# State-space half of an output projection beside an attention: 512 columns of one token tile in eight half pieces, where it was 256 columns of both tiles

## Chip, cores and metric

One core of one Trainium2 chip. The metric is the device time of one launch in microseconds (us), the median of several runs. Engines: TensorE (PE in the profile, its weight loads apart as PEld), VectorE (DVE), ScalarE (ACT), GpSimd (POOL) and SyncE (SP), which issues the weight loads from HBM.

## What is computed

Two transformer blocks on 256 tokens of width 1024. The second block's mixer is the one that matters here:

```python
u = h @ w_in[l]
y_ssd = ssd_mixer(u_ssd, ...)            # 256 x 1024, state-space half
y_mla = mla_mixer(u_mla, positions, ...) # 256 x 1024, 16-head latent attention
x = x + jnp.concatenate([y_ssd, y_mla], axis=-1) @ w_out[l]   # w_out: 2048 x 1024
x = x + memory_attention(rmsnorm(x, ...), rmsnorm(mem, ...), ...)
```

The product with `w_out` is split by rows. Rows 0 to 1023 meet `y_ssd` (layer `out_ssd` of the kernel), rows 1024 to 2047 meet `y_mla` (layer `out_mla`). `y_ssd` is ready before the attention runs, so `out_ssd` can be computed between the steps of the attention.

## The kernel before

**Numbers.** A float32 product is made of three reduced-precision products: `product` (L2253) issues hi x hi (L2256), hi x lo (L2257) and lo x hi (L2258). The stationary operand (128 x 128) is a k tile of the tokens of one token tile, the moving operand is a stretch of a weight row tile. The 256 tokens are two tiles t of 128; the 1024 rows are eight k tiles r.

**Weights** come in units of 2048 elements per partition, in one global order (`LAYERS`), through a ring of three raw buffers. For each unit k SyncE issues two loads, ScalarE rounds it to `w_hi` (`split`, the instruction at L687, semaphore `rounded`) and VectorE forms `w_lo = raw - w_hi` (L1494, semaphore `resid`). TensorE waits for `resid >= k + 1` before it uses unit k, and signals `unit_used` with the last matmul on it. The rounded copies too live in three buffers: the four units of `out_ssd`, 96 to 99, lie in buffers 0, 1, 2, 0 and the first two of `out_mla` in 1, 2. ScalarE must see a buffer's last unit used before it rounds the next one into it. Below, unit 0 to 3 means the four of `out_ssd`.

**Order.** Each engine's order is written out by hand. TensorE, around the change (L3005 to L3018):

```python
scores(0)
out_ssd(0, 0)
out_ssd(0, 1)
for gi in range(3):
    scores(gi + 1)
    turn_probs(gi)
    out_ssd(gi + 1, 0)
    weighted(gi)
    out_ssd(gi + 1, 1, (lambda: turn_probs(3)) if gi == 2 else None)
weighted(3)
```

Four groups gi of four heads: `scores` (L2636, 16 records), the softmax on ScalarE (`exps`, L953) and VectorE (`row_max` L1769 and L1771, `attn_factors` L1793 and L1798), `turn_probs` (transposes, L2649, 12 records), a copy from PSUM (`prob_T_out`, L1787), `weighted` (L2666, 16 records), a copy (`attn_out`, L1805). `scores(gi)` waits for the exponentials of gi - 1, `turn_probs(gi)` for `rec_ready` of `attn_factors(gi)`, `weighted(gi)` for `prob_T_out(gi)`.

`out_ssd(i, t)` (L2671) computes 256 columns of token tile t over all eight k tiles with unit i alone: 24 matmuls of 256 columns into one half of PSUM bank 7. After both tiles `unit_used` rises; VectorE's `side_add(i)` (L1814) adds the bank to the residual stream `X` in one instruction (two at i = 3) and frees the bank for `out_ssd(i + 1, 0)` through `side_added`. The bank is one for all pieces.

VectorE, same stretch (L2102 to L2129): last transposed inputs, `row_max(0)`, `split(unit 1)`, `side_add(0)`, `attn_factors(0)`; then for gi = 0, 1, 2: `row_max(gi + 1)`, `prob_T_out(gi)`, `split(unit gi + 2)` (at gi = 2: `attn_factors(3)`), `attn_out(gi)`, and for gi < 2 `attn_factors(gi + 1)`, `side_add(gi + 1)`. Then `split(first out_mla unit)`, `prob_T_out(3)`, `attn_out_lo(0)` (L1812), `side_add(3)`, `attn_out_lo(1)`, `(2)`, `attn_out(3)` and what `out_mla` needs. Unit 0 was split earlier.

ScalarE, same stretch: `exps(gi)` and `split(unit gi + 2)` for gi = 0 to 3, a copy for the last group (L1198), then four `mla_out_hi` (L1204), which round the attention's result into `xT_hi`, the buffer in which `out_ssd` still read its tokens; each waits until all of `out_ssd` is done. `out_mla` starts on `o2_lo`, from `attn_out_lo(0)`.

Of the kernel before, what the change touches and what calls it, by code (L numbers as in the profile page):

```python
# [29 lines left out]
ACT = mybir.ActivationFunctionType  # L30
ALU = mybir.AluOpType
# [3 lines left out]
TT = 2  # L35
S = TT * P
D = 1024
KT = D // P
# [32 lines left out]
U0, _n = {}, 0  # L71
# [118 lines left out]
def two_blocks(nc, a, consts, mla_rows, columns, first, out):  # L190
    with ExitStack() as ctx:
# [11 lines left out]
        X = sb("X", [P, TT, D])  # L203
# [138 lines left out]
        def prob_T(gi):  # L342
            return view(9568 + gi % 2 * 1536, 1536)

        ps = ctx.enter_context(nc.psum_tensor("ps", [P, 8, 512], F32))
# [129 lines left out]
        END = {name: U0[name] + n for name, n in LAYERS}  # L475
# [24 lines left out]
        XU = ["f0", "wout", "f1", "out_ssd", "out_mla", "mo", "f2"]  # L500
# [41 lines left out]
        def in2_unit0(n):  # L542

            return U0["in2"] + 2 * n
# [9 lines left out]
        def _(sp):  # L554
            def load(k, dst_src, c=0):

                if not isinstance(c, int) or k + 3 * c >= RING + 2:

                    sp.wait_ge(resid, 3 * c + (k - RING + 1))
                for dst, src in dst_src:  # L560
                    sp.dma_start(dst, src).then_inc(weights_in[k % RING], 16)

            def rows_by_cols(k, w, row_tile, nk, c0, n):

                src = w.rearrange("(k p) n -> p k n", p=P)
                dst = raw[k % RING][:, 0:nk * n].rearrange("p (k n) -> p k n", k=nk)
                h = (nk + 1) // 2
                return [(dst[:, 0:h], src[:, row_tile:row_tile + h, c0:c0 + n]),
                        (dst[:, h:nk], src[:, row_tile + h:row_tile + nk, c0:c0 + n])]
# [54 lines left out]
            k = U0["win"]  # L624
# [7 lines left out]
            for n, c in enumerate(IN2_CHUNKS):  # L632
                k = in2_unit0(n)
# [3 lines left out]
            for i in range(3):  # L637
                k = U0["qup"] + i
                load(k, rows_by_cols(k, a["mla_w_q_up_2"][0], 0, 3, 512 * i, 512))
            for i in range(2):  # L640
                k = U0["kvup"] + i
                load(k, rows_by_cols(k, a["mla_w_kv_up_2"][0], 0, 2, 1024 * i, 1024))
            for i in range(4):
                k = U0["out_ssd"] + i
                if i == 3:
                    sp.wait_ge(scaled, SCALE_FIRST.index("out_ssd") + 1)
                    sp.dma_start(qT2[QK:QK + 2, :, :].rearrange("p a b -> p (a b)"), mla_rows[0]).then_inc(mask_rows_in, 16)
                    sp.dma_start(kT2[QK:QK + 2, :, :].rearrange("p a b -> p (a b)"), mla_rows[1]).then_inc(mask_rows_in, 16)
                load(k, rows_by_cols(k, a["w_out_2"][0], 0, 8, 256 * i, 256))
            two_row_tiles("out_mla", a["w_out_2"][0], (8, 10, 12, 14))  # L650
            two_row_tiles("mk", a["w_mem_k_2"][0])
            two_row_tiles("mv", a["w_mem_v_2"][0])
            for i in range(4):
                k = U0["mq"] + i
# [4 lines left out]
            for t in range(TT):  # L659
                for h, done in enumerate((out_act, out_dve)):  # L660
                    c = slice(512 * h, 512 * h + 512)
# [5 lines left out]
        def _(act):  # L667
# [398 lines left out]
            for n in range(5):  # L1066
                c, b = IN2_CHUNKS[n], IN2_BANKS[n]
# [126 lines left out]
                               ps[0:QK, MT_BANK[j % 4], :].rearrange("p (a b) -> p a b", a=2), ACT.Copy).then_inc(mT_act, 1)  # L1194
            turned("out_ssd", 2, 6)
            attention(0, 4)
            act.wait_ge(pT3_ps, 2)
            act.activation(prob_T(3)[:, 512:1024], ps[:, 4, :], ACT.Copy).then_inc(pT3_act, 1)  # L1198

            def mla_out_hi(gi):  # L1200

                act.wait_ge(o_ready, gi + 1)
                act.wait_ge(unit_used, END["out_ssd"])
                act.activation(xT_hi[:, 2 * gi:2 * gi + 2, :], o2T[:, 2 * gi:2 * gi + 2, :], ACT.Copy).then_inc(o2_hi, 1)  # L1204

            for gi in range(4):
                mla_out_hi(gi)
            for i in range(4):
                split(U0["out_mla"] + i + 2)
                turned("mk", 2 * i, 2)  # L1210
# [261 lines left out]
        def _(dve):  # L1472
# [7 lines left out]
            TTn = nc.vector.tensor_tensor  # L1480
# [6 lines left out]
            def split(k, c=0):  # L1487

                if isinstance(c, int) and k + 3 * c >= UNITS:
                    return  # L1490
                n = width(k) if isinstance(c, int) else UW

                dve.wait_ge(rounded, 3 * c + (k - 1))
                TTn(w_lo[HOME[k]][:, 0:n], raw[k % RING][:, 0:n], w_hi[HOME[k]][:, 0:n].bitcast(F32),  # L1494
                    ALU.subtract).then_inc(resid, 1)
# [293 lines left out]
            def attn_factors(gi):  # L1789

                kind, g, nk, hg, dv = GROUPS[gi]
                dve.wait_ge(p_ready, 2 * gi + 2)
                link(nc.vector.reciprocal(rec[:, gi % 2, :, :], p_sum[:, gi % 2, :, :]))  # L1793
                at = 0
                for t in range(TT):
                    n = nk[t] * P
                    v = prob(gi)[:, at:at + hg * n].rearrange("p (h n) -> p h n", h=hg)
                    last = TTn(v, v, bc(rec[:, gi % 2, t, :], n), ALU.mult)  # L1798
                    at += hg * n
                last.then_inc(rec_ready, 1)  # L1800
# [12 lines left out]

            def side_add(i):  # L1814

                dve.wait_ge(unit_used, U0["out_ssd"] + i + 1)
                c = slice(256 * i, 256 * i + 256)
                if i < 3:
                    TTn(X[:, :, c], ps[:, 7, :].rearrange("p (t n) -> p t n", t=TT), X[:, :, c], ALU.add).then_inc(side_added, 1)
                else:  # L1820
                    for t in range(TT):
                        TTn(X[:, t, c], ps[:, 7, t * 256:t * 256 + 256], X[:, t, c], ALU.add).then_inc(x_ready, 1)

            def rope(dst, src, half, sin, cos, tmp):

# [276 lines left out]
            turned("out_ssd", 2, 6)  # L2102
            row_max(0)
            split(U0["out_ssd"] + 1)
            side_add(0)
            attn_factors(0)
            for gi in range(3):
                row_max(gi + 1)
                prob_T_out(gi)
# [142 lines left out]
        def _(pe):  # L2252
            def product(out_, lhs, rhs, first, last, **kw):  # L2253

                (lh, ll), (rh, rl) = lhs, rhs
                pe.matmul(out_, lh, rh, start=first, stop=False, **kw)  # L2256
                pe.matmul(out_, lh, rl, start=False, stop=False, **kw)  # L2257
                return pe.matmul(out_, ll, rh, start=False, stop=last, **kw)  # L2258

            def xT(k, t):  # L2260
                return xT_hi[:, k, t * P:t * P + P], xT_lo[:, k, t * P:t * P + P]

            def wt(k, at, n):
                return w_hi[HOME[k]][:, at:at + n], w_lo[HOME[k]][:, at:at + n]
# [16 lines left out]
            def xT_there(name, k):  # L2281

                if name in NIDX:
                    pe.wait_ge(xt_lo, kts(name, k + 1))
# [383 lines left out]
                                             start=(kt == 0), stop=(kt == 1), skip_group_check=True)  # L2668
                last.then_inc(o_ps, 1)

            def out_ssd(i, t, between=None):  # L2671

                k = U0["out_ssd"] + i
                if t == 0:
                    pe.wait_ge(resid, k + 1)
                    if i:
                        pe.wait_ge(side_added, i)
                for r in range(KT):
                    if i == 0 and t == 0:
                        xT_there("out_ssd", r)  # L2680
                    if r == 4 and between is not None:
                        between()
                    last = product(ps[:, 7, t * 256:t * 256 + 256], xT(r, t), wt(k, 256 * r, 256), r == 0, r == KT - 1)
                if t == 1:
                    last.then_inc(unit_used, 1)

# [82 lines left out]
            for j in range(4):  # L2769
                for t in range(TT):  # L2770
                    last = pe.transpose(ps[:, 6 + j // 2, j % 2 * S + t * P:j % 2 * S + t * P + P], z1[:, t, PW + j * P:PW + j * P + P], ident)
            last.then_inc(qT1_ps, 1)
            for t in range(TT):
                last = pe.transpose(ps[:, 3, t * P:t * P + P], z1[:, t, 1024:1152], ident)
# [30 lines left out]
            for g in range(4):  # L2805
# [3 lines left out]
                last = pe.matmul(out_[:, P:S], z1[:, 1, g * P:g * P + P], cst[:, at + S:at + S + P], start=False, stop=True,  # L2809
                                 skip_group_check=True)  # L2810
# [5 lines left out]
            for t in range(TT):  # L2816
                for g in range(4):
                    last = pe.matmul(ps[:, t, g * P:g * P + P], dT[:, g, t * P:t * P + P], w_pool_sb[:, g, :],
                                     start=True, stop=True)
# [8 lines left out]
            for n in range(6):  # L2828
                c = IN2_CHUNKS[n]
# [11 lines left out]
                if 0 <= m < 4:  # L2841
# [8 lines left out]
                    for q in range(4):  # L2850
                        for t in range(TT):
                            last = pe.transpose(ps[:, 4 + m % 2 * 2 + q // 2, q % 2 * S + t * P:q % 2 * S + t * P + P],
                                                xbc_in[m % 2][:, t, q * P:q * P + P], ident)
# [22 lines left out]
            for t in range(TT):  # L2876
                for ft in range(8):
                    last = pe.transpose(dn[:, t, ft * P:ft * P + P], xbcT[:, ft, t * P:t * P + P], ident)
# [6 lines left out]
            for g in CB_ORDER:  # L2885
# [3 lines left out]
                for i, (s_, l_) in enumerate(((0, 0), (1, 1), (0, 1))):  # L2889
                    last = pe.matmul(ps[:, g, i * P:i * P + P], xbcT[:, 8 + g, s_ * P:s_ * P + P],  # L2890
                                     xbcT[:, 12 + g, l_ * P:l_ * P + P], start=True, stop=True)
# [74 lines left out]
            for s_ in range(4):  # L2966
                k = U0["kvup"] + s_ // 2
# [6 lines left out]
                for t in range(TT):  # L2974
                    for r in range(2):
                        last = product(ps[:, (2 * s_ + 6 + t) % 8, :], xT(3 + r, t), wt(k, 1024 * r + 512 * (s_ % 2), 512),
                                       r == 0, r == 1)
# [39 lines left out]
            k = U0["out_mla"]  # L3017
            pe.wait_ge(resid, k + 1)  # L3018
            pe.wait_ge(o2_lo, 1)
            for t in range(TT):  # L3020
# [3 lines left out]
                for r in range(2):  # L3024
                    for h in range(2):
                        last = product(dn[:, t, 512 * h:512 * h + 512], xT(r, t), wt(k, 1024 * r + 512 * h, 512),
                                       r == 0, False)
# [123 lines left out]
```

## Time and profile before

| | |
|---|---|
| median of 3 runs | 949.96 us (949.69 to 950.05) |
| the profiled execution's own time | 950.72 us |
| its span, first to last instruction | 948.9 us |
| busy: PE, DVE, ACT, POOL | 940.2 (99%), 658.8 (69%), 611.7 (64%), 100.7 us (11%) |
| mean granted TensorE clock | 0.998 |
| the stretch of the change | about 582.7 to 626.0 us of the span |

A row of a timeline gives start, duration, engine, line, operation, output and input names, sizes and count; in brackets, where there are any, the engine's idle time before it and what ended it. Matmul records overlap: their duration includes filling and draining the array, so the pace of TensorE is read from the distance between starts. The records of VectorE overlap by a little too (about 0.08 us).

### The profile page before, as it was taken

The numbers are of one execution on the slowest core, as the hardware profiler recorded it, in microseconds if no ns is written. First come the engines' busy times: TensorE is split into PE (matmuls) and PEld (weight loads), VectorE is DVE, ScalarE is ACT, GpSimd is POOL, SyncE is SP. The second block draws the span as 40 slices with busy tenths as digits, with TensorE's granted clock in tenths as the row PEclk, the third lists the DMA queues.
The fourth block names the chain that finished last, engine by engine and source line by source line (L and its number), as shares of the span: only waits on it lengthen the run. The fifth ranks groups of instructions, "written<-read, shape, count | busy, mean of one in ns | idle before, by whom it ended". The sixth has DMA issues, their size and how long they took to land.

```text
span 948.9 us, 14225 instructions
## 1 busy us (share of the span) xinstructions
PE 940.2 (99%) x5156; PEld 800.6 (84%) x5156; DVE 658.8 (69%) x817; ACT 611.7 (64%) x1046; POOL 100.7 (11%) x132
## 2 busy tenths in 40 slices
PE   9999999999999999999999999999999999999997
PEld 8888888887888888887889789989899898888886
DVE  5656565675675555657679898886566668787887
ACT  6786867666667777686557596554454475666654
POOL 0026600010010000000101923000000010000000
PEclk9999999999999999999999999999999999999999
DMA  9777655633446565655545253244652537465641
GB/s 349 244 231 230 221 184 196 216 134 112 161 155 207 179 208 177 221 177 178 185 134 200 78 180 135 90 154 154 221 181 90 178 106 236 149 219 176 199 155 45
DMA packets 107715, 167.08 MB, mean 176 GB/s; under 512 B 5444, under 2 KB 80372, under 8 KB 107540
## 3 DMA queue, kind: packets, MB, share of 16 engines
q1 hardware_dynamic: 106264, 161.57, 50.8%
q0 software_dynamic: 1408, 4.93, 1.8%
q8 instruction: 28, 0.46, 0.2%
q14 instruction: 15, 0.12, 0.0%
HBM read 165.43 MB, written 1.05 MB: 175 GB/s over the span
## 4 chain that ended last, share of the span: by engine, by line
PE 97%; ACT 1%; DVE 1%; issue 0%; POOLq 0%; POOL 0%; ACTq 0%; DVEq 0%
PE ps L2256 26%; PE ps L2258 25%; PE ps L2257 25%; PE ps L2529 6%; PE ps L2535 3%; PE ps L2636 1%; PE ps L2295 1%; PE ps L2991 1%; PE ps L2276 1%; PE ps L2649 1%; PE ps L2689 1%; PE ps L2927 1%; PE ps L2666 0%; PE ps L2307 0%; PE ps L2332 0%; PE ps L2310 0%
## 5 line engine op out<-in xcount | busy, mean ns | idle before, releaser
L1494 DVE TENSOR_TENSOR w_lo<-raw,w_hi 128x2048 fp32r<-128x2048 f32 (+2 forms) x140 | 316.8, 2273 | 77.0 <-ACT w_hi L687 76.9
L687 ACT ACTIVATE w_hi<-raw 128x2048 fp32r<-128x2048 f32 (+2 forms) x140 | 263.0, 1888 | 36.5 <-PE ps L2258 30.9
L2256 PE MATMUL ps<-w_hi,xT_pair 128*128 128x512 f32 (+2 forms) x706 | 268.2, 380 | 0.3
L2258 PE MATMUL ps<-w_hi,xT_pair 128*128 128x512 f32 (+2 forms) x706 | 264.4, 375 | 0.0
L2257 PE MATMUL ps<-w_lo,xT_pair 128*128 128x512 f32 (+2 forms) x706 | 264.1, 374 | 0.0
L2256 PEld LDWEIGHTS ps<-w_hi,xT_pair 128*128 128x128 f32 x706 | 132.9, 188 | 24.3 <-issue 2.1
L2258 PEld LDWEIGHTS ps<-w_hi,xT_pair 128*128 128x128 f32 x706 | 132.8, 188 | 23.7
L2257 PEld LDWEIGHTS ps<-w_lo,xT_pair 128*128 128x128 f32 x706 | 133.0, 188 | 22.1
L906 ACT ACTIVATE arena<-arena 32x128 f32<-32x128 f32 x288 | 88.5, 307 | 4.4 <-DVE arena L1616 1.3
L2257 PE MATMUL ps<-w_lo,hT_hi 128*128 128x512 f32 x224 | 87.2, 389 | 0.0
L2258 PE MATMUL ps<-w_hi,hT_lo 128*128 128x512 f32 x224 | 87.2, 389 | 0.0
L2256 PE MATMUL ps<-w_hi,hT_hi 128*128 128x512 f32 x224 | 87.2, 389 | 0.0
L2529 PE MATMUL ps<-xT_pair,w_hi 128*128 128x512 f32 x256 | 79.0, 395 | 0.0
L834 ACT ACTIVATE arena<-ps,rstd 128x256 f32<-128x256 f32 x44 | 20.7, 473 | 60.3 <-PE ps L2258 57.5
L1736 DVE TENSOR_TENSOR hT_lo<-arena,hT_hi 128x512 fp32r<-128x512 f32 x18 | 12.5, 694 | 62.0 <-ACT hT_hi L910 62.0
L2256 PE MATMUL ps<-xT_pair,w_hi 128*128 128x256 f32 x192 | 54.6, 285 | 0.0
L2258 PE MATMUL ps<-xT_pair,w_lo 128*128 128x256 f32 x192 | 54.3, 283 | 0.0
L2257 PE MATMUL ps<-xT_pair,w_hi 128*128 128x256 f32 x192 | 54.3, 283 | 0.0
L2535 PEld LDWEIGHTS ps<-xT_pair,w_lo 128*128 128x128 f32 x256 | 45.8, 188 | 9.8
L2258 PEld LDWEIGHTS ps<-w_hi,hT_lo 128*128 128x128 f32 x224 | 42.1, 188 | 8.8
L2257 PEld LDWEIGHTS ps<-w_lo,hT_hi 128*128 128x128 f32 x224 | 42.1, 188 | 8.7
L2256 PEld LDWEIGHTS ps<-w_hi,hT_hi 128*128 128x128 f32 x224 | 42.0, 188 | 8.7
(357 smaller groups left out, 1338.7 us busy)
## 6 DMA issues: line engine op xcount, KB each, us to landing
raw<-in_ffn_w_gu SPq DMA_DIRECT2D x80, 512.0 KB, 4.7
raw<-in_ffn_w_down SPq DMA_DIRECT2D x44, 512.0 KB, 3.9
raw<-in_w_ffn_up SPq DMA_DIRECT2D x44, 512.0 KB, 4.8
raw<-in_w_in SPq DMA_DIRECT2D x34, 512.0 KB, 4.6
raw<-in_w_out SPq DMA_DIRECT2D x24, 512.0 KB, 4.3
raw<-in_w_ffn_down SPq DMA_DIRECT2D x22, 512.0 KB, 4.3
raw<-in_w_mem_k SPq DMA_DIRECT2D x8, 512.0 KB, 4.3
raw<-in_w_mem_v SPq DMA_DIRECT2D x8, 512.0 KB, 4.3
```

The lines of the kernel that those rows point to most:

```text
L687: act.activation(w_hi[HOME[k]][:, 0:n], raw[k % RING][:, 0:n], ACT.Copy).then_inc(rounded, 1)
L834: act.activation(silu_g[:, t, :], ps[:, b, 0:FC], ACT.Silu, scale=rstd[:, t, 0:1]).then_inc(silu_done, 1)
L906: last = act.activation(to[:, a_], rows_[:, b_], ACT.Copy)
L1494: TTn(w_lo[HOME[k]][:, 0:n], raw[k % RING][:, 0:n], w_hi[HOME[k]][:, 0:n].bitcast(F32), ALU.subtract).then_inc(resid, 1)
L1736: TTn(hT_lo[:, :, :], h_raw[:, :, :], hT_hi[:, :, :].bitcast(F32), ALU.subtract).then_inc(hT_lo_done, 1)
L2256: pe.matmul(out_, lh, rh, start=first, stop=False, **kw)
L2257: pe.matmul(out_, lh, rl, start=False, stop=False, **kw)
L2258: return pe.matmul(out_, ll, rh, start=False, stop=last, **kw)
L2276: ins = pe.transpose(ps[:, TURN_BANK[name] + k // 2, k % 2 * S + t * P:k % 2 * S + t * P + P], src[:, t, c:c + P], ident)
L2295: pe.transpose(turn_at(name, t, k), X[:, t, k * P:k * P + P], ident).then_inc(xt_ps, 1)
L2529: ins = pe.matmul(ps[:, (0, 2, 1, 3)[q], :], wt(k + half, 512 * r + P * q, P)[0], pair(kt), start=(kt == 0), stop=(kt == KT - 1))
L2535: ins = pe.matmul(ps[:, (0, 2, 1, 3)[q], S:2 * S], wt(k + half, 512 * r + P * q, P)[1], xT_hi[:, kt, :], start=False, stop=False, skip_gro ...
```

## The change

`out_ssd(i, half)` now computes 512 columns of one token tile over four k tiles. Its calls and their order stay. Token tile is `i % 2`, the column half is `i // 2`; unit `2 * (i // 2) + half` holds 512 columns of k tiles 0 to 3 (half 0) or 4 to 7 (half 1). A piece is 12 matmuls of 512 columns; two halves fill bank 7. Units 0 and 1 serve i = 0 and 1, units 2 and 3 serve i = 2 and 3. `side_add` moves behind `attn_factors` for i = 0, waits for the first tile of the next scores for i < 3, and adds one token tile's 512 columns. On ScalarE two `mla_out_hi` move ahead of the copy at L1198.

```diff
-                load(k, rows_by_cols(k, a["w_out_2"][0], 0, 8, 256 * i, 256))
+                load(k, rows_by_cols(k, a["w_out_2"][0], 4 * (i % 2), 4, 512 * (i // 2), 512))
...
+            def mla_out_hi(gi):
+
+                act.wait_ge(o_ready, gi + 1)
+                act.wait_ge(unit_used, U0["out_ssd"] + (3 if gi < 2 else 4))
+                act.activation(xT_hi[:, 2 * gi:2 * gi + 2, :], o2T[:, 2 * gi:2 * gi + 2, :], ACT.Copy).then_inc(o2_hi, 1)
+
+            mla_out_hi(0)
+            mla_out_hi(1)
             act.wait_ge(pT3_ps, 2)
             act.activation(prob_T(3)[:, 512:1024], ps[:, 4, :], ACT.Copy).then_inc(pT3_act, 1)
-
-            def mla_out_hi(gi):
-
-                act.wait_ge(o_ready, gi + 1)
-                act.wait_ge(unit_used, END["out_ssd"])
-                act.activation(xT_hi[:, 2 * gi:2 * gi + 2, :], o2T[:, 2 * gi:2 * gi + 2, :], ACT.Copy).then_inc(o2_hi, 1)
-
-            for gi in range(4):
-                mla_out_hi(gi)
+            mla_out_hi(2)
+            mla_out_hi(3)
...
             def side_add(i):
 
-                dve.wait_ge(unit_used, U0["out_ssd"] + i + 1)
-                c = slice(256 * i, 256 * i + 256)
+                t, c = i % 2, slice(512 * (i // 2), 512 * (i // 2) + 512)
                 if i < 3:
-                    TTn(X[:, :, c], ps[:, 7, :].rearrange("p (t n) -> p t n", t=TT), X[:, :, c], ALU.add).then_inc(side_added, 1)
+                    dve.wait_ge(sc_ps, 2 * (i + 1) + 1)
                 else:
-                    for t in range(TT):
-                        TTn(X[:, t, c], ps[:, 7, t * 256:t * 256 + 256], X[:, t, c], ALU.add).then_inc(x_ready, 1)
+                    dve.wait_ge(unit_used, U0["out_ssd"] + 4)
+                TTn(X[:, t, c], ps[:, 7, :], X[:, t, c], ALU.add).then_inc(side_added if i < 2 else x_ready, 1)
...
             split(U0["out_ssd"] + 1)
+            attn_factors(0)
             side_add(0)
-            attn_factors(0)
...
-            def out_ssd(i, t, between=None):
-
-                k = U0["out_ssd"] + i
+            def out_ssd(i, half, between=None):
+
+                t, c = i % 2, i // 2
+                k = U0["out_ssd"] + 2 * c + half
                 if t == 0:
                     pe.wait_ge(resid, k + 1)
-                    if i:
-                        pe.wait_ge(side_added, i)
-                for r in range(KT):
-                    if i == 0 and t == 0:
-                        xT_there("out_ssd", r)
-                    if r == 4 and between is not None:
+                if half == 0 and 0 < i < 3:
+                    pe.wait_ge(side_added, i)
+                elif half == 0 and i == 3:
+                    pe.wait_ge(x_ready, 2 * XU.index("out_ssd") + 1)
+                for r in range(4):
+                    if i == 0:
+                        xT_there("out_ssd", 4 * half + r)
+                    if r == 2 and between is not None:
                         between()
-                    last = product(ps[:, 7, t * 256:t * 256 + 256], xT(r, t), wt(k, 256 * r, 256), r == 0, r == KT - 1)
+                    last = product(ps[:, 7, :], xT(4 * half + r, t), wt(k, 512 * r, 512), half == 0 and r == 0,
+                                   half == 1 and r == 3)
                 if t == 1:
                     last.then_inc(unit_used, 1)
```

## Rows read from the trace of the kernel before

**Rows 1.** The page: the chain by engine; then the core's span and mean granted clock.
```profile
PE 97%; ACT 1%; DVE 1%; issue 0%; POOLq 0%; POOL 0%; ACTq 0%; DVEq 0%
...
core 0: 948.9 us, clock 0.998
```

**Rows 2.** Windows, one pass: length, busy PE, PEld, DVE, ACT, POOL, clock, DMA.
```profile
600.30:611.60 11.30, 11.30 (x95) 10.45 (x94) 9.43 (x11) 7.42 (x21) 0.86 (x2) 1.00 0.28 108
```

**Rows 3.** Timeline of TensorE, from the first piece to the third.
```profile
582.66 0.47 PE L2256 MATMUL ps<-w_hi,xT_pair 128*128 128x256 f32 x1
582.97 0.28 PE L2257 MATMUL ps<-w_lo,xT_pair 128*128 128x256 f32 x1
...
588.47 0.28 PE L2258 MATMUL ps<-w_hi,xT_pair 128*128 128x256 f32 x1
588.59 2.78 PE L2636 MATMUL ps<-arena 98*128 98x128 f32 x16
591.51 1.53 PE L2649 MATMUL ps<-cst,arena 128*128 128x128 f32 x12
592.79 0.36 PE L2256 MATMUL ps<-w_hi,xT_pair 128*128 128x256 f32 x1
```

**Rows 4.** Timeline of VectorE, over the first and the second pass.
```profile
585.82 2.28 DVE L1494 TENSOR_TENSOR w_lo<-raw,w_hi 128x2048 fp32r<-128x2048 f32 x1
...
589.62 1.83 DVE L1798 TENSOR_TENSOR arena<-arena,rec 128x512 f32<-128x512 f32 x2
...
601.36 0.69 DVE L1769 TENSOR_REDUCE mx<-ps 128x4 f32<-128x512 f32 x1 [0.20 <-PE ps L2636]
...
603.09 1.22 DVE L1769 TENSOR_REDUCE mx<-ps 128x4 f32<-128x1024 f32 x1 [0.83 <-PE ps L2636]
...
606.09 2.28 DVE L1494 TENSOR_TENSOR w_lo<-raw,w_hi 128x2048 fp32r<-128x2048 f32 x1
```

**Rows 5.** The chain that ended last, in the stretch of the change.
```profile
625.84 0.14 issue
```

**Rows 6.** Timeline of TensorE: the last group's L2666, then matmuls of 512 columns.
```profile
624.31 1.52 PE L2666 MATMUL ps<-arena 128*64 128x256 f32 x16
625.98 0.47 PE L2256 MATMUL ps<-w_hi,xT_pair 128*128 128x512 f32 x1
...
628.80 0.39 PE L2256 MATMUL ps<-w_hi,xT_pair 128*128 128x512 f32 x1
...
631.29 0.39 PE L2258 MATMUL ps<-w_hi,xT_pair 128*128 128x512 f32 x1
...
631.88 0.49 PE L2256 MATMUL ps<-w_hi,xT_pair 128*128 128x512 f32 x1
...
634.73 0.39 PE L2256 MATMUL ps<-w_hi,xT_pair 128*128 128x512 f32 x1
```

**Rows 7.** Timeline of TensorE, the pass of gi = 1.
```profile
600.26 2.78 PE L2636 MATMUL ps<-arena 98*128 98x128 f32 x16
602.88 1.48 PE L2649 MATMUL ps<-cst,arena 128*128 128x128 f32 x12
604.12 0.36 PE L2256 MATMUL ps<-w_hi,xT_pair 128*128 128x256 f32 x1
...
607.16 1.52 PE L2666 MATMUL ps<-arena 128*64 128x256 f32 x16
608.61 0.39 PE L2256 MATMUL ps<-w_hi,xT_pair 128*128 128x256 f32 x1
...
611.59 2.78 PE L2636 MATMUL ps<-arena 98*128 98x128 f32 x16
```

**Rows 8.** Timeline of ScalarE, end of the last pass.
```profile
617.69 1.92 ACT L687 ACTIVATE w_hi<-raw 128x2048 fp32r<-128x2048 f32 x1
622.55 0.60 ACT L1198 ACTIVATE arena<-ps 128x512 f32<-128x512 f32 x1 [2.94 <-PE ps L2649]
...
624.48 1.67 ACT L1204 ACTIVATE xT_pair<-arena 128x512 fp32r<-128x512 f32 x3 [1.32 <-PE ps L2258]
```

## Prediction, written before the changed kernel ran

> **What bounds the kernel now.** I read the chain by engine first: TensorE makes up 97% of it, at a mean granted clock of 0.998 [rows 1]. So a change pays only by what it takes from TensorE's own sequence of starts, and costs whatever makes TensorE wait. Then one pass of the stretch by windows: over 11.30 us TensorE is busy throughout while VectorE has 9.43 and ScalarE 7.42 us of work [rows 2]; both have slack inside a pass, though VectorE has under 2 us. Then the timelines of three engines, where the order of instructions and the distances between them can be read [rows 3, 4, 6 to 8].
>
> **The matmuls.** Before, eight pieces of 24 matmuls of 256 columns: 192. After, eight pieces of 12 of 512 columns: 96. The pace is read from starts. At 256 columns, from 582.97 to 588.47 are 46 steps, so 119.6 ns each [rows 3]. At 512 columns, from 628.80 to 631.29 are 11 steps, so 226.4 ns [rows 6]. The same columns cost 239.2 ns in two and 226.4 ns in one: a fixed 12.8 ns saved for each matmul that goes, 12 to a piece, 0.15 us a piece. Whole pieces bound this: before 2.98 us (608.61 to 611.59) and 3.04 us (604.12 to 607.16) [rows 7]; twelve 512-column matmuls take 2.82 us after a pause and 2.85 us after transposes [rows 6]. That gives 0.16 and at most 0.19 us; the last gap before L2666 may remain, so the lower end is 0.10. I take 0.15.
> The Trainium skill (TensorE: Matmul & The Clock Gate, section Back-to-back issue gap) gives columns over 2.4 GHz plus 2.5 ns. By it the fixed part would be 2.5 ns and the saving 0.03 us a piece, which would put my sum 0.7 us higher. The rows disagree with it, 12.8 ns against 2.5, and I go by the rows.
>
> **The unit that is needed early.** This is the largest term. Before, both first pieces used unit 0, and unit 1 was first needed at 592.79, by `out_ssd(1, 0)` [rows 3]. After, `out_ssd(0, 1)` is half 1 and needs unit 1 right behind the first piece. The diff moves `attn_factors(0)` ahead of `side_add(0)`, but `split(unit 1)` on VectorE stays behind `row_max(0)`: it runs from 585.82 for 2.28 us, to 588.10 [rows 4].
> Step by step: the first piece starts at 582.66 as before [rows 3] and takes 2.85 us, so TensorE is through at 585.5. Unit 1 is there at 588.10. A matmul released by VectorE starts 0.14 us after the record's end [rows 5], at 588.24. TensorE idles 2.7 us. The second piece takes 2.82 us and `scores(1)` starts at 591.06. Before it started at 588.59 [rows 3]: **2.47 us late**. The stall is bounded by 0.06 to 0.25 us for the release in place of 0.14, so 2.4 to 2.6 late.
>
> **What the late start gives back at once.** `scores` occupies TensorE 2.62 us (600.26 to 602.88 [rows 7]), so before, `scores(1)` was through at 591.21, but the transposes started at 591.51 [rows 3]: TensorE waited 0.30 us for `attn_factors(0)`, which came behind `side_add(0)` and ran from 589.62 for 1.83 us [rows 4]. After, the factors start when unit 1 is split, near 588.1, and are done near 590.2, long before `scores(1)` ends at 593.7. The 0.30 us goes, and another 0.04 us by which the transposes after that wait took longer (591.51 to 592.79 against 602.88 to 604.12 [rows 3, 7]). `out_ssd(1, 0)` starts 2.13 us late. From there six pieces are 0.15 shorter: minus 0.90. Left at the end of the last piece: 1.23.
>
> **The second unit.** `out_ssd(2, 1)` now needs unit 3 where it had needed unit 2, which had long been there. VectorE splits unit 3 from 606.09 for 2.28 us, to 608.37, and may release TensorE at 608.51. TensorE came there at 608.61 and will come 0.15 earlier, at 608.46, both times counted within the pass [rows 4, 7]. Cost 0.05 us. The bounds: nothing, and one `side_add` of 0.6 us if that pushes VectorE's pass back.
>
> **The adds on VectorE.** `side_add(1)` and `(2)` now wait for the first tile of the scores instead of the piece just finished. Queued behind each are `row_max`, the copy, the next split; ScalarE's exponentials and TensorE's transposes wait for those. In the pass of gi = 1 the first maximum starts at 601.36, when that tile is there; now the add of 0.6 us goes first. But the second maximum waited 0.83 us for its own tile, until 603.09 [rows 4]. Shifted by 0.6, the first maximum and its small successor are through near 602.85, 0.2 us before. So nothing on the path, and 0.6 us a pass if that cover were gone. For i = 0 the add comes at about 592.1, its bank is needed at 594.9. The last add in one instruction of 512 columns instead of two is worth nothing: VectorE has time there.
>
> **ScalarE.** The `w_hi` buffer of unit 0 is now free only after `out_ssd(1, 0)`, so `split(unit 3)` on ScalarE may wait about half a microsecond; the next exponentials come 5 us later and cover it. The buffer of unit 2 is in use until `out_ssd(3, 0)` ends, near 618.6; the split of the second `out_mla` unit ran from 617.69 and moves to 618.7. The two early `mla_out_hi` come behind it, some 0.6 us each (three take 1.67), to 621.9, and the copy L1198 starts at 622.55 [rows 8]. They fit with 0.6 us to spare; without that cover `weighted(3)` would wait. What they bring: the chain shows TensorE waiting for ScalarE's and VectorE's rounding after the last piece. `mla_out_hi(0)` no longer stands there. `weighted` takes 1.45 us (607.16 to 608.61 [rows 7]); the last one starts at 624.31, so TensorE would have been free at 625.76 and started at 625.98 [rows 6]. Minus 0.22 us.
> The loads: eight k tiles of 256 columns become four of 512, as many bytes, longer runs, the same queue and order, no other issue moved past another. Unit 1 and unit 3 are loaded long before VectorE splits them. Cost nothing; covered by the ring, and if it were not, a load would show ahead of L687.
>
> **The sum.** +2.47 - 0.34 - 0.90 + 0.05 - 0.22 = +1.06 us. Behind the stretch TensorE stays the bound and the other engines arrive relatively earlier, so the shift is kept to the end. The profiled execution took 950.72 us, 0.76 above the median of 949.96; the sum applies to either: 951.8 for the profiled one and **951.0 as the median**. That is +0.11%. A measurement of this kernel tells about 0.2%, 1.9 us, from no change, so my forecast is within it.
>
> **Rivals.**
> *The adds push the passes back (slower).* Place: `side_add` before `row_max` on VectorE in three passes. For it: only 0.2 us separate the shifted maximum from its successor [rows 4], and VectorE is busy 9.43 of 11.30 us [rows 2]. Against: TensorE itself does not wait for the maximum inside the pass. Price 0.6 us a pass, so +1.06 + 1.8 = +2.9, 952.9 us. It decides from the point where 0.85 us in sum reach TensorE. Chance 0.08.
> *The clock falls after the pause (slower).* The 2.7 us pause would be longer than any in the trace. The only loss of clock the rows show is 0.002 of 948.9 us, 1.9 us in all [rows 1]; if the pause brings back the lower of the two levels (1.2 instead of 2.4 GHz) for as long, the sum is +1.06 + 1.9 = +3.0, 952.9 us. Chance 0.07.
> The Trainium skill (TensorE: Matmul & The Clock Gate, section Why this matters for your kernels) advises against pauses between bursts, because a long enough one brings the engine back to the half-rate clock. No pause in this trace is long enough to test it, and the rival stands on the first sentences.
> *The early need is hidden (faster side).* If unit 1 were ready by 585.5, both first pieces are shorter by 0.31, the transposes follow the scores at once, and the rest stays: -0.31 - 0.34 - 0.90 + 0.05 - 0.22 = -1.7, 948.2 us. Against: VectorE's order, which is fixed, and no gap before 585.82 to pull the split into. Chance 0.08.
> *The longer matmuls don't pay.* Without the 0.90, the sum is +1.96, 951.9 us. Against: the two paces [rows 3, 6]. Chance 0.05.
>
> **The numbers.** Forecast as worked out: 0.72, its own range by the bounds: 2.4 to 2.6 late, pieces 0.10 to 0.19 (0.6 to 1.14 in all), unit 3 0 to 0.6, the end 0 to 0.25. Lowest 2.4 - 0.34 - 1.14 - 0.25 = +0.67, highest 2.6 - 0.34 - 0.6 + 0.6 = +2.26. With 0.3 us for the spread of the runs, 950.3 to 952.5. That holds the rival of the longer matmuls too; a little of the others is needed for eight in ten, so 950.0 to 952.6. Of the 0.72, 0.05 lies above +1.9 us. Slower: 0.05 + 0.08 + 0.07 + 0.03 of the last rival = 0.23. Faster by over 0.2%: 0.03, from the hidden need with luck. Same: 0.74.
>
> **What would show it.** Right: one idle time of TensorE of about 2.7 us before L2256 near 588, ended by VectorE's L1494; none before L2649; starts in the pieces 0.23 us apart, a pass of about 11.0 us; `out_mla` starting near 627.0. Wrong: a second pause before the piece of unit 3, a `row_max` of a second tile that starts without waiting for TensorE, matmuls of 512 columns that start 0.43 us apart after the pause, or no pause at all.

## Result and profile after

| | before | changed |
|---|---|---|
| median of 13 runs each | 950.13 us | 951.74 us |
| lowest, highest | 949.69, 950.60 | 951.04, 953.15 |
| ratio, 95% interval | | 1.0019 (1.0012 to 1.0027) |
| profiled execution: its time, span | 950.72, 948.9 us | 951.40, 949.6 us |

The change costs 1.6 us. The runs of the changed kernel also lie further apart than those of the kernel before, 2.1 us against 0.9.

The page of the changed kernel and its core row:

```profile
span 949.6 us, 14031 instructions
...
PE 938.8 (99%) x5060; PEld 794.4 (84%) x5060; DVE 658.9 (69%) x816; ACT 612.1 (64%) x1046; POOL 100.8 (11%) x132
...
core 0: 949.6 us, clock 0.999
```

TensorE has 96 instructions fewer and 1.4 us less of busy time (940.2 before), while the span grew: the time went into TensorE standing still. Its waits in the stretch:

```profile
PE ps L2257 <- DVE w_lo L1496: 2.4, 1, 2.4
```

One wait, 2.4 us, for the residual of a weight unit (L1496 is L1494 of before, L2257 is L2256; the other lines move by one to four in the same way, and by more in the kernels below). Where it stands, in TensorE's timeline of the changed kernel, against [rows 3]:

```profile
582.07 0.58 PE L2257 MATMUL ps<-w_hi,xT_pair 128*128 128x512 f32 x1
...
584.76 0.39 PE L2259 MATMUL ps<-w_hi,xT_pair 128*128 128x512 f32 x1
587.57 0.50 PE L2257 MATMUL ps<-w_hi,xT_pair 128*128 128x512 f32 x1 [2.41 <-DVE w_lo L1496]
...
590.43 2.78 PE L2637 MATMUL ps<-arena 98*128 98x128 f32 x16
593.05 1.48 PE L2650 MATMUL ps<-cst,arena 128*128 128x128 f32 x12
594.28 0.47 PE L2257 MATMUL ps<-w_hi,xT_pair 128*128 128x512 f32 x1
...
597.22 1.52 PE L2667 MATMUL ps<-arena 128*64 128x256 f32 x16
598.67 0.50 PE L2257 MATMUL ps<-w_hi,xT_pair 128*128 128x512 f32 x1
...
601.53 2.78 PE L2637 MATMUL ps<-arena 98*128 98x128 f32 x16
...
608.32 1.52 PE L2667 MATMUL ps<-arena 128*64 128x256 f32 x16
609.77 0.50 PE L2257 MATMUL ps<-w_hi,xT_pair 128*128 128x512 f32 x1
...
625.17 1.52 PE L2667 MATMUL ps<-arena 128*64 128x256 f32 x16
626.62 0.50 PE L2257 MATMUL ps<-w_hi,xT_pair 128*128 128x512 f32 x1
```

This execution reached the first piece 0.59 us earlier than the one of before (582.07 against 582.66), so distances from the first piece are compared. `scores(1)` comes at 8.36 us (5.93 before), 2.43 us late. The third piece comes at 12.21 (10.13), 2.08 late. The attention's own projection starts at 44.55 (43.32), 1.23 late. The span is 0.7 us longer although the stretch was reached 0.59 us earlier: 1.3 us in all. Counted by starts, the second piece begins 2.81 us after the last start of the first (584.76 to 587.57) where the ordinary distance is 0.23, so the wait takes 2.58 us of TensorE's sequence; the profile shows 2.41 because the last record runs on.

VectorE's timeline of the changed kernel, in the first pass and the second:

```profile
585.23 2.28 DVE L1496 TENSOR_TENSOR w_lo<-raw,w_hi 128x2048 fp32r<-128x2048 f32 x1
587.50 0.20 DVE L1795 RECIPROCAL rec<-p_sum 128x8 f32<-128x8 f32 x1
...
602.62 0.69 DVE L1823 TENSOR_TENSOR X<-ps,X 128x512 f32<-128x512 f32 x1 [1.17 <-PE ps L2637]
603.23 0.68 DVE L1771 TENSOR_REDUCE mx<-ps 128x4 f32<-128x512 f32 x1
...
604.35 1.22 DVE L1771 TENSOR_REDUCE mx<-ps 128x4 f32<-128x1024 f32 x1 [0.23 <-PE ps L2637]
```

Unit 1 is split behind the first group's maxima as before, and TensorE starts 0.06 us after the record ends. The add goes ahead of the first maximum; the second still waits 0.23 us for its tile, so the add costs the path nothing.

So 1.3 us are explained by this trace, and 1.6 were measured in the median. The runs hold more than the trace: of the 13, eight had a mean granted clock of 0.998 or 0.999 and took 951.04 to 951.88 us, five had 0.996 or 0.997 and took 952.58 to 953.15. The eight have a median of 951.56, 1.4 us above the kernel before, so the five lift the median of all by only 0.2 us. The 67 runs of the kernel before beside the experiments below had 0.998 or 0.999 throughout, but for one of 0.948 that took 951.4 us. The experiments ask two things: is the late unit the whole of the 1.3 us, and does the pause cost clock on top.

### The profile page after: what moved, and what is told of

Same layout as the page of the kernel before. It is cut to its first block, busy times and chain, and to the rows that moved or that the text cites. A ratio compares the mean times of both kernels' runs of the same rounds, so it can differ in the third digit from the quotient of the medians.

```text
span 949.6 us, 14031 instructions
## 1 busy us (share of the span) xinstructions
PE 938.8 (99%) x5060; PEld 794.4 (84%) x5060; DVE 658.9 (69%) x816; ACT 612.1 (64%) x1046; POOL 100.8 (11%) x132
## 4 chain that ended last, share of the span: by engine, by line
PE 97%; ACT 1%; DVE 1%; issue 0%; POOLq 0%; POOL 0%; DVEq 0%
PE ps L2257 26%; PE ps L2259 25%; PE ps L2258 25%; PE ps L2530 6%; PE ps L2536 3%; PE ps L2637 1%; PE ps L2296 1%; PE ps L2277 1%; PE ps L2996 1%; PE ps L2667 1%; PE ps L2650 1%; PE ps L2694 1%; PE ps L2932 1%; PE ps L2333 0%; PE ps L2308 0%; PE ps L2334 0%
## 5 line engine op out<-in xcount | busy, mean ns | idle before, releaser
L1496 DVE TENSOR_TENSOR w_lo<-raw,w_hi 128x2048 fp32r<-128x2048 f32 (+2 forms) x140 | 316.9, 2274 | 77.4 <-ACT w_hi L687 77.3
L2257 PE MATMUL ps<-w_hi,xT_pair 128*128 128x512 f32 (+2 forms) x674 | 262.8, 390 | 2.5 <-DVE w_lo L1496 2.4
L2259 PE MATMUL ps<-w_hi,xT_pair 128*128 128x512 f32 (+2 forms) x674 | 258.9, 384 | 0.0
L2258 PE MATMUL ps<-w_lo,xT_pair 128*128 128x512 f32 (+2 forms) x674 | 258.5, 384 | 0.0
L2257 PEld LDWEIGHTS ps<-w_hi,xT_pair 128*128 128x128 f32 x674 | 126.6, 188 | 28.2 <-DVE w_lo L1496 3.0
L2259 PEld LDWEIGHTS ps<-w_hi,xT_pair 128*128 128x128 f32 x674 | 126.6, 188 | 25.0
L2258 PEld LDWEIGHTS ps<-w_lo,xT_pair 128*128 128x128 f32 x674 | 126.7, 188 | 23.0
L2257 PE MATMUL ps<-w_hi,hT_hi 128*128 128x512 f32 x224 | 87.2, 389 | 0.0
L2257 PE MATMUL ps<-xT_pair,w_hi 128*128 128x256 f32 x192 | 54.6, 285 | 0.0
L2257 PEld LDWEIGHTS ps<-w_hi,hT_hi 128*128 128x128 f32 x224 | 42.1, 188 | 8.8
```

## Experiments

Medians and ratios are against runs of the kernel before on the same chip: 950.20 us for the first four kernels, 949.99 for the next four, 950.36 for the last three.

### The order of two VectorE steps alone

```diff
             split(U0["out_ssd"] + 1)
-            side_add(0)
             attn_factors(0)
+            side_add(0)
```

On the kernel before.

> The kernel before with one part of the change: on VectorE attn_factors(0) stands ahead of side_add(0). Theory (one late unit sets the loss): TensorE's wait of 0.30 us ahead of the transposes of the first group goes, and nothing else moves: 0.3 us less than before. Rival (the pause of 2.4 us changes the clock in some executions): no pause here, so the same 0.3 us less, and runs as close together as those of the kernel before (within 1 us of each other), granted clock 0.998 or more in all.

Measured: 949.74 us, ratio 0.9996 (0.9987 to 1.0005), eleven runs within 1.2 us, clock 0.998 or 0.999 in all. The trace has no wait of TensorE in the stretch. The median is 0.46 us lower where 0.3 was forecast, but the interval reaches over 1, so the runs alone don't show a gain.

### The early need of unit 1 taken away

```diff
+                wk = U0["out_ssd"] if i == 0 else k
-                if t == 0:
-                    pe.wait_ge(resid, k + 1)
+                if t == 0 or k == U0["out_ssd"] + 1:
+                    pe.wait_ge(resid, wk + 1)
...
-                    last = product(ps[:, 7, :], xT(4 * half + r, t), wt(k, 512 * r, 512), half == 0 and r == 0,
+                    last = product(ps[:, 7, :], xT(4 * half + r, t), wt(wk, 512 * r, 512), half == 0 and r == 0,
```

> The changed kernel, but the second half of the first token tile multiplies with unit 0 again instead of unit 1 (that part of the product is another than the reference's), so the same matmuls run and unit 1 is first needed one call later. Theory: TensorE's pause of 2.4 us goes, and 0.3 us of the two first pieces, 0.34 us ahead of the transposes, three passes shorter by 0.23 and 0.22 at the end are left as gains: 1.5 us less than before, near 948.6. Rival of the clock: the same minus 1.5 in the median, and no second group of runs at a clock of 0.996. If the 512-column matmuls brought nothing, it would be 0.6 us less than before.

Measured: 948.82 us, ratio 0.9985 (0.9976 to 0.9994), that is 1.4 us less than before; clock 0.998 or 0.999 in all eleven. This kernel leaves out the product of unit 1 with the first token tile: unit 0 stands in for it. As many matmuls of the same size run, and for the time only the moment at which unit 1 is needed differs from the changed kernel, and a loss of 1.6 us becomes a gain of 1.4. The longer matmuls and the other parts of the change pay.

### The wait alone, without the longer matmuls

```diff
-            side_add(0)
             attn_factors(0)
+            side_add(0)
...
                     if i:
                         pe.wait_ge(side_added, i)
+                elif i == 0:
+                    pe.wait_ge(resid, k + 2)
```

On the kernel before; `out_ssd(0, 1)` computes what it did.

> The kernel before with attn_factors(0) ahead of side_add(0), and TensorE waiting for unit 1 ahead of its second piece though that piece does not use it: the wait alone, without the longer matmuls. Theory: a pause of 2.4 us at the same place, scores(1) 2.7 us late, 0.34 back at the transposes: 2.4 us more than before. Rival of the clock: the runs fall into two groups about 1.2 us apart, the upper one with a granted clock lower by 0.002 to 0.003, as those of the changed kernel; by the theory alone they lie within 1 us.

Measured: 953.85 us, ratio 1.0035 (1.0021 to 1.0048), 3.65 us more and not 2.4. One of five runs had a clock of 0.999 and took 952.64, 2.4 us more, as forecast. The four others had 0.996 or 0.997 and took 953.53 to 954.13. The profiled execution is one of these. The end of its pause, and its windows of 1 us (columns as in [rows 2], the granted clock third from the end):

```profile
587.64 0.38 PE L2256 MATMUL ps<-w_hi,xT_pair 128*128 128x256 f32 x1 [2.29 <-DVE w_lo L1494]
```

```profile
586.00:587.00 1.00, 0.00 (x0) 0.00 (x0) 1.00 (x1) 1.00 (x7) 0.00 (x0) 1.00 0.99 401
...
588.00:589.00 1.00, 1.00 (x11) 1.00 (x10) 1.00 (x2) 1.00 (x1) 0.00 (x0) 0.92 0.53 98
589.00:590.00 1.00, 1.00 (x6) 1.00 (x6) 0.64 (x1) 0.34 (x1) 0.00 (x0) 0.50 0.93 287
590.00:591.00 1.00, 1.00 (x7) 1.00 (x6) 0.00 (x0) 0.00 (x0) 0.00 (x0) 0.50 1.01 410
591.00:592.00 1.00, 1.00 (x7) 1.00 (x7) 0.00 (x0) 0.00 (x0) 0.00 (x0) 0.50 0.66 270
592.00:593.00 1.00, 1.00 (x9) 1.00 (x9) 0.69 (x1) 0.00 (x0) 0.00 (x0) 0.87 0.00 0
```

The pause ends at 587.64. TensorE runs at 2.4 GHz for 1.2 us more; then the granted clock is 0.50, that is 1.2 GHz, for some 3.4 us, and 1.00 again. The full-clock execution took what the wait alone was forecast to cost, and the others 0.9 to 1.5 us more. So the clock is no rival but a second part of the loss, and this kernel shows it without the longer matmuls.

### The residual of unit 1 on GpSimd

```diff
             TTp(h1, t4[0], t4[1], ALU.subtract).then_inc(rope2_done, 1)
+            k = U0["out_ssd"] + 1
+            pool.wait_ge(rounded, k - 1)
+            pool.wait_ge(resid, k)
+            TTp(w_lo[HOME[k]][:, :], raw[k % RING][:, :], w_hi[HOME[k]][:, :].bitcast(F32),
+                ALU.subtract).then_inc(resid, 1)
...
-            split(U0["out_ssd"] + 1)
             attn_factors(0)
             side_add(0)
+            dve.wait_ge(resid, U0["out_ssd"] + 2)
```

On the changed kernel, with nothing left out.

> The changed kernel with the residual of unit 1 formed on GpSimd, behind its last rope instruction (that ends at 576.6), instead of on VectorE. Four times 512 elements at the 1.78 us of its other such instructions make 7.1 us, ready at about 583.8, before TensorE asks for it at 585.5. Theory: no pause, as e2: 1.5 us less than before, all of the product computed. If GpSimd takes over 9 us for it, TensorE waits for the rest; if it slows VectorE's rounding of the inputs beside it, the first pieces start later and the gain shrinks below 1 us. Rival of the clock: no second group of runs.

Measured: **948.70 us**, ratio 0.9984 (0.9975 to 0.9993), 1.5 us less than before; clock 0.998 or 0.999 in all eleven runs. GpSimd's and TensorE's timelines of this kernel:

```profile
573.95 1.78 POOL L1453 TENSOR_TENSOR arena<-arena 128x512 f32<-128x512 f32 x1
575.69 4.55 POOL L1457 TENSOR_TENSOR w_lo<-raw,w_hi 128x2048 fp32r<-128x2048 f32 x1
```

```profile
581.75 0.58 PE L2262 MATMUL ps<-w_hi,xT_pair 128*128 128x512 f32 x1
...
584.45 0.39 PE L2264 MATMUL ps<-w_hi,xT_pair 128*128 128x512 f32 x1
584.68 0.39 PE L2262 MATMUL ps<-w_hi,xT_pair 128*128 128x512 f32 x1
...
587.40 2.78 PE L2642 MATMUL ps<-arena 98*128 98x128 f32 x16
```

GpSimd took 4.55 us for the residual where 7.1 was forecast. It is there at 580.24, 4.4 us before it is needed, and the second piece follows the first at the ordinary distance of 0.23 us. `scores(1)` comes 5.65 us after the first piece. The changed kernel has 8.36, so there the late unit costs 2.71 us, nearly all of it the 2.58 lost by the wait and the 0.14 by which the piece behind it takes longer (2.86 us against 2.72). This version beats both kernels; its gain over the kernel before is 0.16%, small, but the interval leaves 1 out.

### The changed kernel again

> The changed kernel once more. Theory as it stands now: a late unit costs 1.3 us in every run (951.4), and in a part of the runs the granted clock falls to half behind the pause of 2.4 us, as the trace of e3 shows, for another 1.2 to 1.5 us. So two groups of runs, one at 951.0 to 951.9 with a granted clock of 0.998 to 0.999, one at 952.6 to 953.2 with 0.996 to 0.997. Rival: the wide spread was of the first chip, and these runs lie within 1 us.

Measured: 951.88 us, ratio 1.0021 (1.0012 to 1.0030). Six runs at 0.998 or 0.999: 951.05 to 951.88. Five at 0.996 or 0.997: 952.17 to 953.25. The two groups are there, on another chip. The gap between them is smaller than forecast (0.3 us); their medians, 951.45 and 952.74, are 1.3 us apart.

### The pause doubled

```diff
             row_max(0)
+            k = U0["out_ssd"] + 1
+            dve.wait_ge(rounded, k - 1)
+            link(TTn(w_lo[HOME[k]][:, :], raw[k % RING][:, :], w_hi[HOME[k]][:, :].bitcast(F32), ALU.subtract))
             split(U0["out_ssd"] + 1)
```

> The changed kernel with VectorE's residual of unit 1 formed twice, the first time in vain, so TensorE's pause grows from 2.4 to 4.7 us. By the late unit alone: 2.3 us more than a2, 953.8, and runs within 1 us. With the clock: the fall comes in nearly every run and not in some, another 1.2 us or more, 955 to 956, granted clock 0.996 or less in nearly all.

Measured: 955.67 us, ratio 1.0059 (1.0045 to 1.0073), all five runs at 0.994 to 0.997, from 955.42 to 956.03. The profile has one wait of 4.7 us, and the clock falls 0.3 us before it ends:

```profile
589.00:590.00 1.00, 0.00 (x0) 0.00 (x0) 1.00 (x1) 0.52 (x1) 0.00 (x0) 0.92 0.00 0
590.00:591.00 1.00, 0.85 (x2) 0.76 (x3) 0.97 (x4) 0.00 (x0) 0.00 (x0) 0.50 0.00 0
```

The clock stays at 0.50 until 593.3. The median is 4.2 us above the full-clock group of the changed kernel on this chip (951.45): 2.3 for the longer pause, the rest, 1.9, for the clock. All five runs lost the clock, as forecast, though three of them have a mean of 0.997 where 0.996 or less was expected.

### The two early roundings on ScalarE put back

```diff
-            mla_out_hi(0)
-            mla_out_hi(1)
             act.wait_ge(pT3_ps, 2)
             act.activation(prob_T(3)[:, 512:1024], ps[:, 4, :], ACT.Copy).then_inc(pT3_act, 1)
+            mla_out_hi(0)
+            mla_out_hi(1)
```

All four wait for the last piece again.

> The changed kernel with ScalarE's two mla_out_hi back behind the copy and behind the last piece. By the prediction's step on the end of the stretch: 0.22 us more than a2, 951.6 in the group of full clock; TensorE starts out_mla 0.2 us later against the last L2667. If that move did nothing, the two agree; the two groups of runs stay.

Measured: 952.74 us, ratio 1.0025 (1.0015 to 1.0035), but six of nine runs had the lower clock. The three of full clock have a median of 951.73, 0.28 us above the full-clock group of the changed kernel on this chip (951.45), with few runs on either side. The trace is clearer:

```profile
625.38 1.52 PE L2667 MATMUL ps<-arena 128*64 128x256 f32 x16
627.05 0.47 PE L2257 MATMUL ps<-w_hi,xT_pair 128*128 128x512 f32 x1
```

From the last L2667 to `out_mla` it is 1.67 us, as in the kernel before (624.31 to 625.98 [rows 6]), where the changed kernel has 1.45 (625.17 to 626.62): 0.22 us, the term of the prediction.

### The unit split in two halves

```diff
+            k = U0["out_ssd"] + 1
+            dve.wait_ge(rounded, k - 1)
+            for part in range(2):
+                c = slice(1024 * part, 1024 * part + 1024)
+                TTn(w_lo[HOME[k]][:, c], raw[k % RING][:, c], w_hi[HOME[k]][:, c].bitcast(F32),
+                    ALU.subtract).then_inc(resid if part else wa_factor0, 1)
-            split(U0["out_ssd"] + 1)
```

TensorE's part of the edit isn't printed: it waits for `wa_factor0` ahead of the first k tile of `out_ssd(0, 1)` and for `resid` ahead of the third.

> The changed kernel with VectorE forming the residual of unit 1 in two halves of 1024 elements, each with its own signal, and TensorE waiting for each ahead of its two k tiles. The pause shrinks by the second half's 1.1 us to 1.3 us. By the late unit: 1.1 us less than a2's group of full clock, 950.3. With the clock: the short pause no longer costs clock, so the upper group is gone too, and the median falls by more, 1.3 us or so.

Measured: 950.35 us, ratio 1.0002 (0.9993 to 1.0011), eleven runs within 0.4 us, clock 0.998 or 0.999 in all. The wait in the timeline:

```profile
584.59 0.39 PE L2264 MATMUL ps<-w_hi,xT_pair 128*128 128x512 f32 x1
586.40 0.47 PE L2262 MATMUL ps<-w_hi,xT_pair 128*128 128x512 f32 x1 [1.43 <-DVE w_lo L2109]
```

A pause of 1.4 us cost no clock in eleven runs, and the time is 1.1 us below the full-clock group of the changed kernel, as forecast. It still costs a little more than its length: 1.81 us lie between the starts on either side, 1.58 more than the ordinary 0.23.

### The pause filled with work

```diff
                 k = U0["out_ssd"] + 2 * c + half
+                if i == 0 and half:
+                    for _ in range(10):
+                        pe.matmul(ps[:, 3, :], xT_hi[:, 0, 0:P], wt(k - 1, 0, 512)[0], start=True, stop=True)
                 if t == 0:
                     pe.wait_ge(resid, k + 1)
```

> The changed kernel with ten matmuls of 512 columns, whose result nobody reads, between TensorE's first piece and the wait for unit 1. They take 2.3 us and fill the pause without shortening it. By the late unit: nothing gained, 1.3 us more than before in every run. By the clock: TensorE is no longer idle, so the upper group of runs is gone, all lie within 1 us at a granted clock of 0.998 or more, median 951.4, that of the lower group of a2. If the upper group has another cause than the idle time, it stays.

Measured: 951.51 us, ratio 1.0012 (1.0003 to 1.0021), eleven runs from 950.96 to 951.76, clock 0.998 or 0.999 in all. Its timeline:

```profile
582.42 0.58 PE L2257 MATMUL ps<-w_hi,xT_pair 128*128 128x512 f32 x1
...
585.33 2.43 PE L2678 MATMUL ps<-w_hi,xT_pair 128*128 128x512 f32 x10
587.91 0.50 PE L2257 MATMUL ps<-w_hi,xT_pair 128*128 128x512 f32 x1 [0.16 <-DVE w_lo L1496]
...
590.82 2.78 PE L2637 MATMUL ps<-arena 98*128 98x128 f32 x16
```

And a window over the wait, with the clock at 1.00:

```profile
586.00:588.00 2.00, 1.84 (x9) 1.21 (x7) 2.00 (x2) 2.00 (x9) 0.00 (x0) 1.00 1.03 414
```

`scores(1)` comes 8.40 us after the first piece, as late as in the changed kernel (8.36), yet the upper group of runs is gone. The unit is as late as before and only TensorE's idleness is taken away, so the idleness is what costs the clock. With the clock kept, the change as a whole costs 1.15 us here: the late unit less what the rest of the change gains.

### Two more executions of the changed kernel

> The changed kernel, one look, for a profile of an execution of the upper group. Five in ten: the windows behind the pause show a granted clock of 0.5 for about 3 us and starts of 512-column matmuls 0.43 us apart, and the span is 1.2 us or more longer than where they don't.

Measured: 951.23 us, clock 0.999, no fall behind the pause.

> The changed kernel, one more look, with the same expectation as the one ahead of it: a granted clock of 0.5 behind the pause in about half of such executions.

Measured: 952.78 us, and this execution lost the clock. Its core row, windows and TensorE's timeline:

```profile
core 0: 951.0 us, clock 0.996
```

```profile
587.00:588.00 1.00, 0.61 (x3) 0.52 (x4) 0.96 (x3) 1.00 (x3) 0.00 (x0) 0.99 0.53 213
588.00:589.00 1.00, 1.00 (x4) 0.81 (x3) 1.00 (x2) 1.00 (x1) 0.00 (x0) 0.50 0.71 131
589.00:590.00 1.00, 1.00 (x3) 0.77 (x3) 0.39 (x1) 0.09 (x1) 0.00 (x0) 0.50 0.90 319
590.00:591.00 1.00, 1.00 (x4) 0.74 (x3) 0.00 (x0) 0.00 (x0) 0.00 (x0) 0.50 1.03 410
591.00:592.00 1.00, 1.00 (x6) 0.81 (x5) 0.00 (x0) 0.00 (x0) 0.00 (x0) 0.80 0.45 180
```

```profile
581.90 0.59 PE L2257 MATMUL ps<-w_hi,xT_pair 128*128 128x512 f32 x1
...
587.39 0.50 PE L2257 MATMUL ps<-w_hi,xT_pair 128*128 128x512 f32 x1 [2.41 <-DVE w_lo L1496]
...
588.78 0.63 PE L2258 MATMUL ps<-w_lo,xT_pair 128*128 128x512 f32 x1
589.21 0.63 PE L2259 MATMUL ps<-w_hi,xT_pair 128*128 128x512 f32 x1
...
591.85 2.78 PE L2637 MATMUL ps<-arena 98*128 98x128 f32 x16
```

The pause is the same 2.41 us. The matmuls behind it start 0.43 us apart instead of 0.23, and `scores(1)` comes 9.95 us after the first piece, where the first profile of this kernel has 8.36: 1.59 us more, all of it inside one piece. The spans differ by 1.4 us (951.0 against 949.6). The clock falls 0.6 us after the pause has ended and is at half for 3.4 us, summed over the windows.

## Why the prediction came out as it did

The median of 951.74 us lies in the range of 950.0 to 952.6 and 0.7 us above the forecast 951.0; as a difference to the kernel before, whose median over 13 runs is 950.13 and not 949.96, it is 1.6 us where 1.06 was forecast. Point by point:

- **The late unit** (+2.47): 2.43 in the trace, and taking the early need away turned the loss into a gain of 1.4 us. Right in place, cause and size, with a little luck in the size: the release took 0.06 us and not 0.14, and the piece behind it 2.86 and not 2.82.
- **What comes back at the transposes** (-0.34): the third piece is 2.08 late, so 0.35 came back. Right.
- **The shorter pieces** (-0.90): mis-sized. From the third piece to the end the lateness falls from 2.08 to 1.23, of which 0.22 belong to the end, so six pieces gave 0.63, 0.105 each where 0.15 was taken. **The step that failed** is that steady spacing was taken for whole pieces: the first starts in a piece are further apart at 512 columns (0.34 us behind L2667 and some 0.234 us for the next few) than the steady 0.226. The whole pieces set beside it were not alike either: the 3.04 us of before end with 0.21 us ahead of L2666, and the 2.85 of 512 columns end in one more such matmul at 0.22, where the changed kernel has 0.32 ahead of L2667. Measured on the same places, a piece behind the transposes falls from 3.04 to 2.94 us, and one behind L2667 from 2.98 to 2.86, so 0.10 and 0.12. The prediction had this gap in mind only for its lower bound of 0.10.
- **The second unit** (+0.05): nothing. `out_ssd(2, 1)` follows L2667 by 1.45 us (608.32 to 609.77), as the same piece does in the first pass (597.22 to 598.67).
- **The end** (-0.22): right, shown by the kernel that puts it back. The copy behind the two early roundings still waits 0.90 us for TensorE, so they fit, as said.
- **The adds**: off the path, as said; 0.23 us of cover left.

The sum by the trace is +1.23 at the start of `out_mla` and +1.3 over the span, instead of +1.06. The full-clock runs of the 13 lie 1.4 us above the kernel before, and the clock brings the median to 1.6; the 0.1 us between trace and full-clock runs stays open. **The second step that failed** is that the clock was made a rival with a chance of 0.07, to happen or not. It happens in a part of the executions: of all 26 runs of the changed kernel, eleven had 0.996 or 0.997. Their median is 952.76 us; that of the fifteen others is 951.55. So it costs 1.2 us where it happens (priced at 1.9), and as fewer than half of the 13 runs were hit, their median still lies in the lower group. That the median came out inside the range is partly luck for this reason: with more than half of the runs hit it would lie in the upper group, near 952.8, as that of the kernel with the late roundings does (952.74, six of nine hit). What spoke for this rival was that the pause was over twice as long as any wait of TensorE in the trace of before (the longest is 1.0 us); "no pause in this trace is long enough to test it" was a reason for a wide chance, not for a small one. By the rule of the Trainium skill named there (TensorE: Matmul & The Clock Gate, section Why this matters for your kernels), a long enough pause between bursts brings the half-rate clock. The traces agree on the effect, with 0.50 behind a pause of 2.3 and 2.4 us, but these pauses are shorter than the ones that the section warns of, and the measurement decides. What sets which executions are hit was not found: the pauses of two executions with different clocks are both 2.41 us.

The rule of the same page on spacing (section Back-to-back issue gap), by which a piece would be only 0.03 us shorter, was put aside for the rows; the measured 0.105 lies between the two, nearer to the 0.15 of the rows.

## What to carry to other kernels

When a product is tiled anew, list for each unit of weights the first instruction that needs it: a tiling with fewer and longer matmuls can need a unit earlier, and here 2.4 us of waiting for one residual ate 1.5 us of gain. The cure was not in the tiling but in who prepares that unit: an engine with an open stretch ahead of the need. And a pause of TensorE like this one has to be priced twice, by its length and by the chance that the clock falls behind it; runs that spread into two groups with different granted clocks are the sign.

## What the runs showed of the hardware

- The three profiled executions with a lowered mean clock (0.996 or 0.997) show 1.2 GHz for 3.4 us around or behind the pause. By the mean clock, it was lost in eleven of 26 runs of the changed kernel (pause of 2.4 us), in six of nine of the one with the late roundings (2.4), and in four of five of the kernel before with the wait alone (2.3); with a pause of 4.7 us in five of five, with one of 1.4 us in none of eleven, and with the pause filled in none of eleven.
- The fall can come after the pause is over: in the kernel with the wait alone TensorE had been busy again for 1.2 us, in the profiled execution of the changed kernel for 0.6 us. With the pause of 4.7 us it came 0.3 us before the end.
- GpSimd subtracted 2048 contiguous elements per partition in 4.55 us, while its rope instruction with a strided operand took 1.78 for 512; four times the latter would have been 7.1.
